# Branch projections as three split products from the common weight stream, in half-size units, with the second norm half shared out

## The reference

```
h = modulate(rmsnorm(x, g1), shift, scale)
p = h @ w_in                                   # q, kv, rope key, 4 pool groups, 4 Fourier groups, 3 gates
attn   = attention of 8 heads (scores, softmax, values)        # 512 wide
pooled = (window mean - itself) @ w_pool * s_pool              # 4 groups of 128
four   = real part of a 2-D FFT                                # 4 groups of 128
y = sigmoid(g0) * (attn @ w_oa) + sigmoid(g1) * (pooled @ w_ob) + sigmoid(g2) * (four @ w_oc)
x = x + gate1 * (y @ w_out)
h = modulate(rmsnorm(x, g2), shift2, scale2)
layer 0: x += gate2 * (silu(h @ w1) * (h @ w3)) @ w2
layer 1: the two best of 8 experts, each such a block; then a final rmsnorm
```

## Time and profile before

| | |
|---|---|
| median of 3 runs | 2039.86 us (2038.47 to 2040.59) |
| profiled execution | 2039.14 us, span 2037.4 us |
| TensorE busy | 1963.6 us, 96% |
| VectorE busy | 1364.3 us, 67% |
| ScalarE busy | 990.8 us, 49% |
| mean granted TensorE clock | 0.978 |
| fp32 branch products (L1838) | 384 instructions, 131.6 us of modelled busy time |

### The profile page before, as it was taken

The page is one execution under the profiler, slowest core; times in us unless marked ns, Lnnn a source line. Parts: engine busy times, 40 slices in busy tenths (PEclk is TensorE's granted clock), DMA queues, the critical chain, the costliest instruction groups (busy, mean ns, idle before and its releaser), DMA issues.

```text
span 2037.4 us, 24090 instructions
## 1 busy us (share of the span) xinstructions
PE 1963.6 (96%) x9008; PEld 1553.9 (76%) x9008; DVE 1364.3 (67%) x1590; ACT 990.8 (49%) x1098; POOL 91.0 (4%) x127
## 2 busy tenths in 40 slices
PE   6999999999899999989999989999999999999997
PEld 3785666667688888868788978888878887888886
DVE  5753444377567646455344568888888888888995
ACT  3423333222522122243434367777767776777774
POOL 0150000000000001002000000000000000000000
PEclk9999999999899999989999979999999999999997
DMA  9312112244255556413233279989988998899980
GB/s 366 127 69 83 42 73 88 88 166 163 96 175 185 187 184 231 176 63 134 83 120 150 94 310 355 355 345 352 347 317 345 352 346 318 345 353 345 355 309 23
DMA packets 72401, 438.76 MB, mean 215 GB/s; under 512 B 9184, under 2 KB 9952, under 8 KB 28000
## 3 DMA queue, kind: packets, MB, share of 16 engines
q1 hardware_dynamic: 60624, 394.18, 51.1%
q0 software_dynamic: 11664, 43.00, 6.0%
HBM read 436.09 MB, written 1.05 MB: 215 GB/s over the span
## 4 chain that ended last, share of the span: by engine, by line
PE 92%; DVE 3%; ACT 2%; issue 2%; DMA 0%; SPq 0%; ACTq 0%; DVEq 0%
PE ps L1605 12%; PE ps L1606 12%; PE ps L1607 12%; PE ps L1993 8%; PE ps L1994 8%; PE ps L1995 8%; PE ps L1838 6%; PE ps L2007 4%; PE ps L2011 4%; PE ps L2008 4%; PE ps L1789 2%; PE ps L1813 2%; PE ps L1748 2%; PE ps L1639 1%; PE ps L1718 1%
## 5 line engine op out<-in xcount | busy, mean ns | idle before, releaser
L1422 DVE TENSOR_TENSOR elo<-estage,ehi 128x2048 fp32r<-128x2048 f32 x264 | 604.9, 2292 | 82.9 <-ACT ehi L933 81.7
L933 ACT ACTIVATE ehi<-estage 128x2048 fp32r<-128x2048 f32 x264 | 505.2, 1914 | 51.3 <-PE ps L2011 47.1
L1605 PE MATMUL ps<-h_hi,whi 128*128 128x512 f32 (+1 forms) x960 | 370.7, 386 | 17.7 <-DVE h_lo L1080 8.8
L1606 PE MATMUL ps<-h_lo,whi 128*128 128x512 f32 (+1 forms) x960 | 347.6, 362 | 0.0
L1607 PE MATMUL ps<-h_hi,wlo 128*128 128x512 f32 (+1 forms) x960 | 347.4, 362 | 0.0
L1993 PE MATMUL ps<-ehi,xg_hi 128*128 128x512 f32 x704 | 288.5, 410 | 8.2 <-issue 3.0
L1994 PE MATMUL ps<-elo,xg_hi 128*128 128x512 f32 x704 | 279.5, 397 | 0.0
L1995 PE MATMUL ps<-ehi,xg_lo 128*128 128x512 f32 x704 | 279.2, 397 | 0.0
L1040 DVE TENSOR_TENSOR wlo<-stage,whi 128x2048 fp32r<-128x2048 f32 x79 | 181.2, 2295 | 98.2 <-ACT whi L675 98.1
L675 ACT ACTIVATE whi<-stage 128x2048 fp32r<-128x2048 f32 x79 | 150.8, 1909 | 164.7 <-PE ps L1607 163.9
L1605 PEld LDWEIGHTS ps<-h_hi,whi 128*128 128x128 f32 x960 | 184.0, 192 | 59.3 <-issue 20.7
(11 more groups left out here) (224 smaller groups left out, 2375.8 us busy)
## 6 DMA issues: line engine op xcount, KB each, us to landing
estage<-in_moe SPq DMA_DIRECT2D x264, 1024.0 KB, 5.0
stage<-in_split SPq DMA_DIRECT2D x79, 1024.0 KB, 4.9
gw<-in_mods POOLq DMA_DIRECT2D x80, 512.0 KB, 3.8
dw<-in_direct SPq DMA_DIRECT2D x36, 512.0 KB, 3.6
mw_b<-in_mods SPq DMA_DIRECT2D x8, 512.0 KB, 12.6
mw_a<-in_early SPq DMA_DIRECT2D x8, 512.0 KB, 14.3
xT<-in_x SPq DMA_DIRECT2D x1, 2048.0 KB, 7.9
gw<-in_cond_rows SPq DMA_DIRECT2D x1, 1024.0 KB, 5.0
```

The costliest lines, as they stand in the source:

```text
L933: act.activation(ehi[:, w % SPLIT, :], estage[:, w % STAGE, :], ACT.Copy).then_inc(S("e_hi_done"), 1)
L1422: dve.tensor_tensor(elo[:, w % SPLIT, :], estage[:, w % STAGE, :], ehi[:, w % SPLIT, :], ALU.subtract)\
L1605: pe.matmul(out, hi, rhs_hi, start=first, stop=False)
L1606: pe.matmul(out, hi, rhs_lo, start=False, stop=False)
```

## The change

The three branch weights leave the direct stream and go through the split stream: each gate tile of 8 blocks is followed by a `proj` tile of 4. The branch inputs `br` become a pair `br_hi`, `br_lo`, and a branch is 4 x 3 fp32r products. The units have 8 blocks instead of 16, with 3 instead of 2 `whi`/`wlo` buffers and still 3 `stage` buffers. The pool weights get a load and a place of their own (`pw`); the direct stream keeps v and the heads, with 2 buffers. In attention `split_hi` is called behind exps and the row copies, `split_lo` behind row_max and head_rope and ahead of merge. In the norms of 512 columns (n1_0, n2_0, n1_1) VectorE scales the second half of each odd tile.

```diff
-SPLIT_BLOCKS = 16
+SPLIT_BLOCKS = 8
-DIRECT = 3
+DIRECT = 2
-DENSE_SPLIT = 2
+DENSE_SPLIT = 3
@@ split_stream
-        tiles += [(("gate", layer, m), KD) for m in range(KD * BRANCHES)]
+        for m in range(NM):
+            tiles += [(("gate", layer, m), KD), (("proj", layer, m), KB)]
@@ Walk
+    def unit_of(self, key, k):
+        return self.block(key, k) // SPLIT_BLOCKS
+    def ahead(self, *key):
+        return self.units_up_to(*key) + DENSE_SPLIT - 1
@@ direct_stream
-        out += [("pool", layer), ("v", layer), ("head", layer, 0)]
...
+        out += [("v", layer)] + [("head", layer, c) for c in range(HEADS // 2)]
@@ shared norm halves
+    def shared(tag, k):
+        return k % 2 == 1 and tag in ("n1_0", "n2_0", "n1_1")
@@ SP
+            if kind == "p":
+                if n == 1:
+                    sp.wait_ge(S("y_lo"), KD)
+                sp.dma_start(pw[:, :, :], A["pool"][n]).then_inc(S("pool_in"), 16)
@@ ScalarE, norm, and the in, out and feed-forward tiles
-                for s, at in parts:
+                for s, at in parts[:1] if shared(tag, k) else parts:
-                split_hi(walk.units_up_to("in", layer, j) + 1)
+                split_hi(walk.ahead("in", layer, j))
@@ ScalarE, gate_tanh and the item loop
-                split_hi(walk.units_up_to("gate", layer, m) + 1)
...
                     for m, half in halves(layer, n):
+                        split_hi(walk.unit_of(("gate", layer, m), KD // 2 * half) + DENSE_SPLIT)
                         if half == 1:
                             gate_tanh(m)
@@ VectorE, norm
+            def second_half(k):
+                if k >= 4:
+                    dve.wait_ge(S("norm_hlo"), KD * nth(tag) + k - 3)
+                dve.wait_ge(S("norm_nt"), KD * nth(tag) + k + 1)
+                dve.tensor_scalar(hslot(k, n)[:, SEQ:T], nt[:, k % 2, SEQ:T], coef[...], mod[...], ALU.mult, ALU.add).then_inc(S("norm_hf2"), 1)
...
                 if k >= 2:
                     lo(k - 2)
+                if shared(tag, k):
+                    second_half(k)
@@ VectorE, Fourier and pool branches
-                    dve.tensor_copy(br[:, 2, g, s * SEQ:(s + 1) * SEQ], ps[4 + n % 2][:, 0:SEQ]).then_inc(S("br_c"), 1)
+                    dve.tensor_copy(br_hi[:, 2, g, ...], ps[4 + n % 2][:, 0:SEQ]).then_inc(S("br_c_hi"), 1)
+                    dve.wait_ge(S("br_c_hi"), earlier("br_c_hi", layer) + n + 1)
+                    dve.tensor_tensor(br_lo[:, 2, g, ...], ps[4 + n % 2][:, 0:SEQ], br_hi[:, 2, g, ...], ALU.subtract).then_inc(S("br_c"), 1)
+            for g in range(GROUPS):
+                dve.wait_ge(S("br_b"), earlier("br_b", layer) + g + 1)
+                dve.scalar_tensor_tensor(br_lo[:, 1, g, lc:T], ps[4 + g % 2][...], s_pool[...], br_hi[:, 1, g, lc:T], ALU.mult, ALU.subtract).then_inc(S("br_b_lo"), 1)
@@ VectorE, head_out
-                dve.tensor_copy(br[at:at + 64, 0, h // 2, lc:T], ps[6][0:64, lc:T]).then_inc(S("br_a"), 1)
+                rows = ps[6][0:64, lc:T]
+                if at:
...
+                    dve.tensor_copy(br_f[64:128, lc:T], rows).then_inc(S("br_a_f"), 1)
...
+                dve.tensor_copy(br_hi[at:at + 64, 0, h // 2, lc:T], rows).then_inc(S("br_a_hi"), 1)
...
+                dve.tensor_tensor(br_lo[at:at + 64, 0, h // 2, lc:T], rows, br_hi[at:at + 64, 0, h // 2, lc:T], ALU.subtract)
@@ VectorE, merge, after_merge and the item loop
-                dve.wait_ge(S("o_full"), earlier("o_full", layer) + m + 1)
+                dve.wait_ge(S("walked"), walk.tile("proj", layer, m))
-                split_lo(walk.units_up_to("gate", layer, m) + 1)
...
                     row_max(n)
                     if n % per == 0 and todo[n][0] + 1 < HEADS:
                         head_rope(todo[n][0] + 1)
+                    for m, half in halves(layer, n):
+                        split_lo(walk.unit_of(("gate", layer, m), KD // 2 * half) + DENSE_SPLIT)
                 if 1 <= n <= len(todo):
                     for m, half in halves(layer, n - 1):
                         if half == 1:
                             merge(m)
@@ TensorE
-                pe.matmul(ps[4 + g % 2][:, 0:T - lc], dw[:, slot, g, :], mixed[:, 0, g, lc:T], start=True, stop=True)\
+                pe.matmul(ps[4 + g % 2][:, 0:T - lc], pw[:, g, :], mixed[:, g, lc:T], start=True, stop=True)\
@@ branch(m), which still waits for o_used of m - 1
                 for k in range(KB):
-                    ins = pe.matmul(ps[1][:, 0:T - lc], dw[:, slot, 4 * (m % 2) + k, :], br[:, b, k, lc:T], start=(k == 0), stop=(k == KB - 1))
-                ins.then_inc(S("o_full"), 1)
+                    block_passes(ps[1][:, 0:T - lc], ("proj", layer, m), k, br_hi[:, b, k, lc:T], br_lo[:, b, k, lc:T], k == 0, k == KB - 1)
```

More of the change, by code:

```diff
@@ L267, in load_order @@
             tile("in", layer, j)
[L269 to L273, removed]
+            if j == 4:
+                add(("p", layer))
+            if j == 8:
+                add(("d", direct_at[("v", layer)]))
+                add(("d", direct_at[("head", layer, 0)]))
+        for m in range(NM):
             tile("gate", layer, m)
@@ L276, in load_order @@
                 add(("d", direct_at[("head", layer, m // 4 + 1)]))
-            add(("d", direct_at[("proj", layer, m // 2)]))
+            tile("proj", layer, m)
         for j in range(KD):
@@ L286, in load_order @@
                     tile("down", half, j)
-    assert len(out) == walk.units + len(direct_at)
+    assert len(out) == walk.units + len(direct_at) + DEPTH
     return out
@@ L491, in direct_used @@
         kind, layer, *rest = direct[n]
-        if kind == "pool":
-            return S("pool_full"), earlier("pool_full", layer) + GROUPS
         if kind == "v":
             return S("v_full"), earlier("v_full", layer) + T // P
-        if kind == "head":
-            return S("qk_full"), qk_full(layer, "q", 2 * rest[0] + 1)
-        return S("o_full"), earlier("o_full", layer) + 2 * (rest[0] + 1)
+        return S("qk_full"), qk_full(layer, "q", 2 * rest[0] + 1)
     def c0(layer):
@@ L881, in _ @@
             for m in range(BESIDE, NM):
+                for half in (0, 1):
+                    split_hi(walk.unit_of(("gate", layer, m), KD // 2 * half) + DENSE_SPLIT)
                 gate_tanh(m)
@@ L888, in _ @@
             for j in range(KD):
-                split_hi(walk.units_up_to("out", layer, j) + 1)
+                split_hi(walk.ahead("out", layer, j))
                 square(f"n2_{layer}", lc, j)
@@ L1172, in _ @@
             for j, name in enumerate(TILES):
-                split_lo(walk.units_up_to("in", layer, j) + 1)
+                split_lo(walk.ahead("in", layer, j))
                 if name == "kr":
@@ L1321, in _ @@
             for j in range(KD):
-                split_lo(walk.units_up_to("out", layer, j) + 1)
+                split_lo(walk.ahead("out", layer, j))
                 if j >= 2:
@@ L1344, in _ @@
                     for i in ks:
-                        split_lo(walk.units_up_to("upu", i) + 1)
+                        split_lo(walk.ahead("upu", i))
                         dve.wait_ge(S("ft"), i + 1)
@@ L1358, in _ @@
                     for j in range(KD):
-                        split_lo(walk.units_up_to("down", half, j) + 1)
+                        split_lo(walk.ahead("down", half, j))
                         if half == 1 and j >= 2:
@@ L1726, in _ @@
                 tokens(n)
-            slot = direct_unit(("pool", layer))
+            pe.wait_ge(S("pool_in"), 16 * (layer + 1))
             for g in range(GROUPS):
@@ L2206, in layout @@
         unit = np.zeros((P, DIRECT_BLOCKS, P), np.float32)
-        if kind == "pool":
-            unit[:, 0:GROUPS] = i["w_pool"][layer].transpose(1, 0, 2)
-        elif kind == "v":
+        if kind == "v":
             v = i["w_ukv"][layer][:, :, NOPE:].reshape(KKV, P, HEADS * VD)
@@ L2221, in layout @@
                     unit[:, 4 * c + 3, x * NOPE:(x + 1) * NOPE] = k[c]
-        else:
-            for x in range(2):
-                j, b = MERGE[2 * key[2] + x]
-                w = i[("w_oa", "w_ob", "w_oc")[b]][layer]
-                unit[:, 4 * x:4 * x + 4] = _blocks(w[:, j * P:(j + 1) * P])[:, 0].transpose(1, 0, 2)
         direct.append(unit)
```

82 lines of the change are left out of this document (52 added, 30 removed).

## The result

| | before | after |
|---|---|---|
| median of the runs side by side, us | 2039.59 (4 runs, 2038.47 to 2040.59) | 2060.24 (4 runs, 2059.69 to 2061.28) |
| ratio, 95% interval | | 1.0102, 1.0084 to 1.0119 |
| span of the profiled execution, us | 2037.4 | 2059.5 |
| mean granted clock of TensorE | 0.978 | 0.972 |

What follows compares the result with a forecast made beforehand. TensorE, nine tenths of the span, was taken as the bound. Terms -16.8 - 2.2 + 25.3 + 11.6 - 1.5 + 2.2 + 1 + 0.4 = +20.0 took the span from 2037.4 to 2057.4, run median 2060 us; range 2036 to 2078.

Steps and rivals of the forecast that it cites:

- Branches: Both layers' 48 branches: 12 split products replace 4 fp32 ones, saving 0.70 us each in layer 0, 0.28 in layer 1; 23.5 total.
- The four passes: Branch products in both layers: three array passes instead of four would save a quarter, 30.9 us in all instead of 23.5.
- The waits ahead of the branch: Layer 1's attention: TensorE waits for VectorE's merge, queued behind the split, 29.8 us lost against 4.5 gained.
- an odd head's three operations: Layer 1's even attention items with an odd head: row_max comes 0.3 us later, making the wait 1.15 us, twice.
- The clock: Layer 1's attention: TensorE's clock halves after waits in eight odd items; 0, 11.6 or 23.2 us, 11.6 taken.
- Rival 2: Layer 1's attention: the waits come but the clock holds, +8.4 us, 2048 us; chance 0.15.
- Layer 0 behind attention, costed at nothing: Layer 0's rounds behind attention: splitting half-size units costs nothing, VectorE going from 64% to 78%; uncovered, 0.7 us a round.
- The norms: Three norms: sharing odd tiles with VectorE starts TensorE 0.5 us earlier each; -1.5 us, bounds -3 to +2.
- The pool: Pool in both layers: extra VectorE operations before the first product and between bank uses; +2.2 us, bounds 0.5 to 4.
- Layer 1's in tiles: Layer 1's in tiles: same lead and queue behind the 3.93 us wait; +1 us, bounds -4 to +3.
- rival 4: Layer 1: 512 KB loads and splits outlast three units; 0.5 us in 58 units, +29 us, 2089 us; chance 0.05.
- Rival 1: Layer 1's attention: merge does not come out, 29.8 and 11.6 us fall away; -21.4, 2018.5 us; chance 0.15.

Runs made afterwards that it cites:

- merge first: Changed kernel with split_lo called behind normalise instead of ahead of merge in the attention items of both layers: 2018.08 us.
- The old kernel with the split first: Kernel before the change with VectorE's split of a unit put ahead of merge, not behind normalise: 2043.01 us.
- the run with nine products: Changed kernel with 9 added products of 512 columns where TensorE waits ahead of the branch in layer 1's odd items 3 to 15: 2048.85 us.
- the version after it: The merge first version with the first half of layer 0 item 17's split issued ahead of the gathered weights' work: 2012.06 us.
- the run with 18 products: Changed kernel with 18 added products of 256 columns where TensorE waits ahead of the branch in layer 1's odd items 3 to 15: 2059.97 us.
- the first run with filled waits: Changed kernel with 20 added products of 256 columns ahead of the gate tile in the 8 odd items of layer 1's attention: 2059.11 us.

## Why the prediction was right, and which of its terms were not

The forecast was 2060.0, the time 2060.24. The mechanism, its place and its size were as it said. That the total agrees within 0.3 us is luck in part: the span grew by 22.1 us and not by 20.0 (the median lies 0.7 us above the span in the kernel after and 2.2 in the one before, for which I had added 2.5), and in the sum several terms were off and cancel.

- **Branches.** -0.70 a branch in layer 0 was right: 8.89 became 8.16, and the items of layer 0's attention are 11.3 us shorter, 11.2 foretold. In layer 1 a round behind attention is 4.32 us from gate to gate (4.60 before), as worked out; in the attention items the branches gave back 3.7 us and not 4.5 (116.7 us before, 113.0 with merge first, first gate to 16th). The four passes of the Trainium skill (FP8 and Floating Point Precision, section TensorE Precision Notes) would have given 7.4 us less in total; layer 0's rounds fell by 0.73, not by 0.86, so the rows were the better source.
- **The waits ahead of the branch.** Predicted 2.95, 2.45, 0.85 to 1.15 and 2.0, measured 2.59, 2.25, 0.56 to 0.83 and 1.64, 25.8 in sum for 29.8. The term was over-sized by 4.0: the odd items' waits were 0.4 and 0.2 shorter, the even ones' 0.0 to 0.4. The 0.3 that I had added for an odd head's three operations doesn't show: the two items with them wait 0.72, their neighbours 0.82. In the odd item shown the scores start at 1026.41; the merge ended 6.53 us later, not 6.8, since two high parts take 1.99 us and not 2.1 and two low ones 2.36 and not 2.46; and TensorE was ready after 4.00 us, not 3.84.
- **Starting again.** A term that was missing: 2.9 us of TensorE's busy time in 15 restarts, 0.19 each. The old kernel with the split first agrees: five waits there, and 117.6 us of busy time from the first gate to the 16th for 116.7, 0.18 each.
- **The clock.** Predicted eight falls at 1.45 us; seven came, at 1.5. Six of them lie in the stage (9.1 us), one behind it. Rival 2, that the clock holds, would have been 2048: the run in which six of the seven falls are taken away and the chain stays as long measures 2048.85, though 1.9 us of that lie where nothing was edited. The Trainium skill (TensorE: Matmul & The Clock Gate, section "HAM oscillation") describes a loop whose wait lowers the clock in each round. The trace agrees in kind, with waits for VectorE in place of DMA: 7 of 8 odd items, one stretch each, never two.
- **Layer 0 behind attention, costed at nothing.** This is the step that failed. It counted VectorE's share (64%, to become 78%) and found room, but what costs is again the order: the low parts of item 17 stand behind mod_units, which waits for gw's transfer, 3.20 us, and one fall of the clock. The gain of 4.9 us in these rounds was lost entirely, and came back in the run with that one split moved. The prediction had asked of the items of layer 1 what is queued behind a waiting instruction, and of layer 0 it had not.
- **Small edits.** The norms let TensorE start 0.49 us earlier each, as said; what it brings in total lies below what the runs can tell. The pool has two waits in each layer (1.07 and 0.80, 1.07 and 0.74) as bounded. Layer 1's in tiles: 3.93 became 4.49 plus a later start, within the bounds. Small units starve (rival 4) is refuted by the run with these alone, 2039.06.
- **Not in the sum.** From layer 0's last gate to its second norm it is 2.3 us less. 0.7 of that is the last branch; for the other 1.6 I had no term: the wait at the start of the out tiles went from 3.15 to 2.80, and one stretch at the lower clock followed in place of two.
- **Rival 1**, the merge does not come out: 2018.5 by the sum. The version in which this holds measures 2018.08. That agreement too is luck in part: the 4.9 us of layer 0's rounds, which the sum counts, are missing in it, and as much came from elsewhere.

By the table of stretches, measured less predicted: start +1.5, layer 0's rounds +4.9, up to layer 1's gates -2.8, layer 1's items -2.7, its last rounds +2.2, the end -0.9. The first can't be read: up to the first gate the experiments' kernels that are the same there took 181.8 to 184.4 us. The items' -2.7 is 4.0 less of waits and 2.5 less of the clock, against 2.9 for starting again and 0.8 that the branches didn't give back. In the last rounds it is the seventh fall (1.6 by the run with nine products, 39.4 us for 41.0) and the start behind the sixteenth item's wait.

## What to carry to other kernels

- When work is added to an engine's queue, don't ask whether the engine has room in the stage, but which release it now stands in front of, and whether its own input is there at that point. VectorE was under half busy (70.9 of 150.9 us) where 38 us were lost; the same operations behind the merge cost nothing, and in the old kernel, ahead of the merge with the input ready, its larger ones cost 3 us.
- A split that comes out of a stream has to be issued behind the short instruction that frees another engine, and ahead of anything that waits for a transfer. Both rules together, the in tiles with them, took the changed kernel from 2060.2 to 2005.4 us.
- A wait put back into a loop costs more than its length: here 25.8 us of waits became 37.8.

## What the chip did that I had not expected

**The clock's sensitivity.** In layer 1's items waits of 2.25 and 2.59 us were followed by a stretch of 3.4 us at 1.2 GHz, seven times in eight; waits of 1.10 and 1.45 us in the same places never were. In the kernel before the shortest wait with a fall behind it that I had shown was 3.04 us. The length of the wait alone doesn't decide: of three waits of 2.25 us two had a fall behind them and one had none, and the wait of 2.81 us behind layer 0's rounds had one with merge first and none in the version after it. What decides between them no run here shows.

**A loop's turn that takes 3 us or 9.** With 126 more matmuls in layer 1, and nothing else moved, TensorE's wait at the turn of the expert loop was 8.84 us in place of 3.10, and the second 6.89 in place of 3.02; with 63 more they were 2.87 and 2.81. But it isn't that a longer program waits longer: the first run with filled waits has 160 more matmuls, and its two waits are ordinary:

```profile
1526.73 0.79 PE L2049 MATMUL ps<-ehi,xg_hi 128*128 128x512 f32 x1 [3.17 <-issue]
1732.04 0.49 PE L2049 MATMUL ps<-ehi,xg_hi 128*128 128x512 f32 x1 [2.94 <-issue]
```

In the 8.84 us wait the table of DMA queues shows two packets on the queue of kind instruction, in the 3.10 us wait of the kernel after one (queue, kind: packets, MB, share):

```profile
q8 instruction: 2, 0.03, 1.3%
...
q8 instruction: 1, 0.02, 1.5%
```

The Trainium skill (Runtime: NRT & Kernel Launch, section "Instruction fetch mechanics") says that a taken branch to code that is not loaded has to fetch it before the engine goes on. The trace agrees in that a packet moves in each of these waits that no engine releases (the 2.81 us one is released by VectorE). The count doesn't give the length, though: the wait of 6.89 us has one packet, like that of 3.10. What makes the turn long in one kernel and short in another stays open; no run here moved the loop alone. For experiments it means that a total can hide an edit's effect: the run with 18 products had saved 9 us in the stage and lost 9.6 in these two waits.
